# A bidirectional RWKV-7 scan on one Trainium2 core: the backward direction's token side moves to the other half of the partitions, and both directions alternate over four quadrants of TensorE

## The chip, the core and the metric

One core of a Trainium2 (trn2) chip runs the whole program. The metric is the time of one execution on the device in microseconds; the version with the lower median is the better one. All arithmetic is float32.

## What is computed

One layer of a diffusion backbone: adaLN-modulated RMSNorm, an input projection, grouped-query attention beside a bidirectional RWKV-7 time mixing, an output projection, and a mixture of experts. The change touches only the scan of the RWKV-7 part. Cut to it, the reference is:

```python
def rwkv7_scan(r, w, k, v, kk, b, s0, reverse):
    def step(S, inp):
        r_t, w_t, k_t, v_t, kk_t, b_t = inp
        sa = jnp.einsum('bhvk,bhk->bhv', S, kk_t)
        S = S * w_t[:, :, None, :] - sa[..., None] * b_t[:, :, None, :] + v_t[..., None] * k_t[:, :, None, :]
        return S, jnp.einsum('bhvk,bhk->bhv', S, r_t)
    ...
y_f, s_f = rwkv7_scan(..., s0[:, 0], False)      # forward
y_b, s_b = rwkv7_scan(..., s0[:, 1], True)       # backward
y = y_f + y_b
```

There are 8 heads of size 64, 128 context tokens and 512 latent tokens, and both directions run over both groups of tokens. The final states of the context tokens are an output.

## The kernel before

The program is a row of blocks that all engines enter together. In the trace the first block (projection) and the second (decays, attention) end at 427.6 us. The scan (lines 1145 to 1614) runs from there to 657.2 us; output projection, routing and experts follow.

**The chunked scan.** The 640 tokens are cut into 10 chunks of C = 64. Each of the ten steps (`STEPS`) treats one chunk of the forward direction (z = 0) and one of the backward direction (z = 1), for all 8 heads: head 2j + p lies in column group j (0 to 3) and partition half p (rows 64p to 64p + 63). Within a chunk the recurrence becomes products of 64 x 64 matrices and one triangular system:

- `gram` (L1290): products of B and of K with A and R, two per head, masked by DVE into `LR` (`lr_out`, L1550) and `MR` (`mr_out`, L1556)
- `turn_kb` (L1299): K and B transposed by a product with the identity, copied by ScalarE into `KB` (L1488)
- `right_sides` (L1340): A times the state plus MR times the values, copied by ScalarE into `RHc` (L1502)
- the triangular system, solved in two halves of 32 tokens: `by_inverse` (L1362), ScalarE's copy `U1` (L1505), `cross` (L1370), DVE's `RHd` (L1591), `by_inverse` again, ScalarE's copy `Uc` (L1513)
- `new_states` (L1381): KB times the values and times Uc; DVE adds the old state and multiplies by the decay (L1599, L1602)
- `outputs` (L1394): R times the state, MR times the values, LR times Uc; DVE adds them into `yacc` (L1609) or copies them (L1611)
- `inner` (L1310), DVE's `z_out` (L1562) and `inverse` (L1326): the inverse of the 32 x 32 triangular blocks of the next step, ScalarE's copy `XTf` (L1492). They need the inverses of the 16 x 16 diagonal blocks, which `diag_blocks` (L1277) gathers for two steps at a time and DVE solves row by row (`solve`, L1530, with `turn_diag` and `turn_back`, L1525 and L1543). Chunks are solved in groups of four, four and two: the first group before step 0, the others within steps 2 and 5.

**Where things lie.** A tile of TensorE is given by the rows that its operands occupy and the partitions that its result goes to. `half(z, p)` says in which half of the partitions the token side of head p lies. It returns p for both directions, so every product of 64 x 64 goes from rows 64p to partitions 64p: only the two quadrants on the diagonal of the array are used. PSUM has eight banks: BG1 = 0 and 1, BG2 = 2 and 3 (forward, backward), BLEV = 4, BDIAG = 5, BSER = 6 and 7.

**What sets the order.** There is no scheduler: each engine executes its list in the order in which it is written, and waits on semaphores. TensorE's list of a step (L1434 to L1473) is: right sides, Gram of B for the next step, first triangular product, Gram of K for the next step, cross, in steps 0, 1 and 4 the diagonal blocks of two more chunks, in step 2 the turned context states, inner for the next step, second triangular product, turned K and B for the next step, new states, outputs, inverse for the next step. Each of these loops treats the forward direction first and then the backward one. DVE's list of a step (L1577 to L1614) begins with `lr_out` of the next step and ends with the outputs; in steps 2 and 5 pieces of the solve stand between, the last piece and `turn_back` behind the outputs. SyncE loads what the next block needs when chunks are done: gates after step 1, half of the output weights after step 3, the bonus after step 4, the attention result after step 7. GpSimd only clears the zero state.

## Time and profile before

| what | value |
|---|---|
| median of 3 runs | 1206.3 us (1205.9 to 1213.83) |
| the profiled execution | 1203.15 us |
| its span, first to last instruction | 1201.3 us |
| mean granted TensorE clock | 0.923 of full speed |
| the scan with its preparation | 427.6 to 657.2 us |
| the ten steps | 458.3 to 657.2 us |

In the profile a matmul of float32 is two records (x2 of what the program issues), each with its weight load (PEld). The stretches below give for each engine the busy time and the number of records in that stretch: PE, PEld, DVE, ACT, POOL, then the granted clock of TensorE as a share of 2.4 GHz, the busy share of the DMA engines and their GB/s. A timeline merges instructions of one line that follow each other; its brackets say how long the engine was idle before and what ended that; "issue" is a wait for nothing that the profile shows.

### The profile page before, as it was taken

To read this page: it belongs to the slowest core of one execution; us is meant where nothing else is said; L and a number is where in the kernel's file an instruction comes from. 1 tells how busy PE (TensorE), PEld (TensorE's weight loads), DVE (VectorE), ACT (ScalarE), POOL (GpSimd) and SP (SyncE) were. 2 spreads that over 40 slices of the span, in tenths; PEclk is the share of its full clock that TensorE was granted. 3 is DMA by queue.
4 is the path that set the end of the run, shared out by engine and by line. 5 is a ranking of instruction groups with operands and counts; after the bars stand their busy time and mean duration, and the time that the engine had idled before them with its cause. 6 is when DMAs were issued, how large, how long until landed. Compare 5 with 4: busy or idle time off the path is not lost. (4 is left out here: it accounts for less than half of the span.)

```text
span 1201.3 us, 22681 instructions
## 1 busy us (share of the span) xinstructions
PE 1032.5 (86%) x9918; PEld 628.6 (52%) x9918; DVE 423.7 (35%) x887; ACT 268.0 (22%) x533; POOL 51.4 (4%) x73
## 2 busy tenths in 40 slices
PE   3699999979888747988899999299999999999960
PEld 0265555525666637887897555244444444444420
DVE  1402642231688653372833664500000010000007
ACT  2311222223676511221122212011111111111100
POOL 0330000010000000000000000300000000000003
PEclk9899999986899877988999999599999999999995
DMA  9713342549998010102101910696899898998816
GB/s 339 232 25 140 110 170 83 200 149 403 408 404 348 10 29 3 39 13 74 47 25 38 323 70 30 246 354 243 311 348 351 306 351 324 334 350 314 311 38 260
DMA packets 95926, 244.82 MB, mean 204 GB/s; under 512 B 6612, under 2 KB 11508, under 8 KB 95328
## 3 DMA queue, kind: packets, MB, share of 16 engines
q1 hardware_dynamic: 85664, 218.64, 50.0%
q0 software_dynamic: 4352, 11.34, 3.0%
q10 hardware_dynamic: 5824, 13.55, 2.9%
q8 instruction: 71, 1.16, 0.4%
q14 instruction: 15, 0.12, 0.0%
HBM read 176.51 MB, written 67.01 MB: 203 GB/s over the span
## 5 line engine op out<-in xcount | busy, mean ns | idle before, releaser
L2104 PE MATMUL ps<-arena 128*128 128x512 f32 x544 | 238.8, 596 | 1.7 <-ACT arena L2154 1.7
L2104 PEld LDWEIGHTS ps<-arena 128*128 128x128 f32 x544 | 102.3, 191 | 126.3 <-issue 125.6
L2118 PE MATMUL ps<-arena 128*128 128x512 f32 x272 | 121.1, 598 | 3.6 <-ACT arena L2158 3.6
L694 PE MATMUL ps<-arena 128*128 128x512 f32 (+3 forms) x448 | 123.6, 435 | 0.0
L694 PEld LDWEIGHTS ps<-arena 128*128 128x128 f32 (+1 forms) x448 | 67.7, 188 | 60.2 <-issue 59.3
L2118 PEld LDWEIGHTS ps<-arena 128*128 128x128 f32 x272 | 50.7, 191 | 61.9 <-issue 61.9
L1773 PE MATMUL ps<-arena 128*128 128x512 f32 x160 | 70.6, 593 | 0.9 <-PEq L1250 0.9
L561 DVE SCALAR_TENSOR_TENSOR arena<-arena 128x128 f32<-128x128 f32 (+3 forms) x56 | 30.9, 552 | 82.6 <-ACT arena L438 81.1
L2195 DVE TENSOR_TENSOR arena<-arena,ps 128x512 f32<-128x512 f32 x17 | 11.7, 689 | 135.5 <-ACT arena L2150 135.5
L2203 DVE COPY arena<-ps 128x512 f32<-128x512 f32 x17 | 11.8, 692 | 125.6 <-PE ps L2118 125.6
L628 PE MATMUL ps<-arena 128*128 128x512 f32 (+1 forms) x160 | 52.4, 485 | 0.0
L598 PE MATMUL ps<-arena 128*32 128x512 f32 x192 | 31.7, 705 | 23.9 <-DMA arena<-in_w_mod_dram 23.9
L2154 ACT ACTIVATE arena<-ps 128x1024 f32<-128x1024 f32 x18 | 18.4, 1024 | 139.9 <-PE ps L2096 139.9
L1773 PEld LDWEIGHTS ps<-arena 128*128 128x128 f32 x160 | 29.5, 189 | 34.8 <-issue 34.8
L2198 DVE TENSOR_TENSOR arena<-arena,ps 128x512 f32<-128x512 f32 x17 | 11.7, 689 | 94.6 <-PE ps L2104 94.6
L1295 PE MATMUL ps<-arena 64*64 64x128 f32 x640 | 40.4, 276 | 3.2 <-issue 3.2
L885 PE MATMUL ps<-arena 128*128 128x128 f32 x160 | 25.4, 291 | 20.1 <-DVE arena L1107 17.5
L628 PEld LDWEIGHTS ps<-arena 128*128 128x128 f32 x160 | 29.9, 189 | 21.5 <-issue 19.3
L1295 PEld LDWEIGHTS ps<-arena 64*64 64x64 f32 x640 | 35.9, 136 | 4.3 <-issue 3.4
L1321 PE MATMUL ps<-arena 32*32 32x32 f32 x640 | 11.6, 228 | 26.0 <-DVE arena L1548 16.1
L2163 ACT ACTIVATE arena<-ps 128x512 f32<-128x512 f32 x17 | 10.2, 597 | 103.0 <-PE ps L2118 103.0
L2096 PE MATMUL ps<-arena 128*128 128x128 f32 x144 | 19.6, 281 | 14.9 <-DMA arena<-gathered_tokens 14.9
(307 smaller groups left out, 1429.7 us busy)
## 6 DMA issues: line engine op xcount, KB each, us to landing
gathered_tokens<-arena SPq DMA_DIRECT2D x16, 2560.0 KB, 27.1
arena<-in_exp_up_dram SPq DMA_DIRECT2D x17, 2048.0 KB, 18.1
arena<-in_exp_gate_dram SPq DMA_DIRECT2D x17, 2048.0 KB, 13.1
arena<-in_exp_down_dram SPq DMA_DIRECT2D x17, 2048.0 KB, 9.8
arena<-in_w_mod_dram SPq DMA_DIRECT2D x12, 2048.0 KB, 13.8
arena<-gathered_tokens SPq DMA_DIRECT2D x18, 512.0 KB, 15.1
expert_outputs<-arena ACTq DMA_DIRECT2D x17, 512.0 KB, 8.1
arena<-in_w_in_dram SPq DMA_DIRECT2D x4, 2048.0 KB, 7.9
```

Source lines behind the costliest of these rows:

```text
L561: ins = dve.scalar_tensor_tensor(o[:, a:b], r_[:, base + off:base + off + b - a], mu[0:m, k, e:e + 1], o[:, a:b], ALU.mult, ALU.add)
L598: mm = pe.matmul(ps[32 * g:32 * g + 32, bank, :], cond32[:, k, :], ring[:, slot_of(what), k, :], start=(k < 4), stop=(k >= 4))
L628: mm = pe.matmul(ps[:, b + half, 0:w], hT[:, k, tt * P:(tt + 1) * P], ring[:, slot_of(("qkv", half)), k, 0:w], start=(k == 0), stop=(k == ...
L694: mm = pe.matmul(ps[0:m, b, 0:hi - lo], ring[:, slot_of(what), k, (e % 4) * P:(e % 4) * P + m], hT[:, k, lo:hi], start=(k == 0), stop=(k = ...
L885: mm = pe.transpose(ps[:, 4 + y // 4, (y % 4) * P:(y % 4 + 1) * P], prob[:, g, y * P:(y + 1) * P], ident)
L1295: mm = pe.matmul(ps[q:q + 64, bank + z, j * 2 * C:(j + 1) * 2 * C], kinds(k, z, s, j, p), kinds(A_, z, s, j, p, 2), start=True, stop=True)
L1773: mm = pe.matmul(ps[:, b, :], catT[k4][:, j, tt * P:(tt + 1) * P], wout[:, half, NC4 * k4 + j, :], start=(k4 == 0 and j == 0), stop=(k4 == ...
L2096: mm = pe.transpose(ps[:, XT0 + k // 4, (k % 4) * P:(k % 4 + 1) * P], xg[:, u, k * P:(k + 1) * P], ident)
L2104: mm = pe.matmul(ps[:, b, :], xgT[:, k, :], w[u][:, k, :], start=(k == 0), stop=(k == KT - 1))
L2118: mm = pe.matmul(ps[:, Y0 + half, :], hidT[:, k, :], wd[u][:, k, half * 512:(half + 1) * 512], start=(k == 0), stop=(k == 3))
L2154: act.activation(xgT, ps[:, XT0:XT0 + 2, :].rearrange("p b (k t) -> p (b k) t", t=P), ACT.Copy).then_inc(xgT_ok, 1)
L2203: dve.tensor_copy(yo[:, u, 512:], ps[:, Y0 + 1, :]).then_inc(yo_v, 1)
```

## The change

- `half(z, p)` becomes `p ^ z`: everything of the backward direction that has tokens on the partitions lies in the other half. Products from rows p to the token side, and from the token side to the state side, of the backward direction now use the two quadrants off the diagonal.
- `gram`, `turn_kb` and `new_states` run both directions in one loop over j, the two diagonal products first and then the two others.
- The right side of the backward direction is split: A times the state goes to BSER + 1; MR times the values is a piece of its own, `swapped_values`, written to BDIAG ahead of the inverse of the step before, copied by ScalarE to `MV1`, and added by DVE, as DVE's first instruction of a step.
- The outputs of the backward direction are split in the same way over two banks: DVE adds two pieces where it added one. Both directions' outputs alternate in one loop, and the backward ones are done two products before the forward ones.
- The values of the backward direction are copied to the other half by GpSimd's DMA queue, two DMAs a step into two buffers (`Vs`).
- Diagonal blocks write one bank for each direction, in steps 0, 1 and 4 the banks BG1 and BG1 + 1 in place of BDIAG, with waits for `lr_ok` before and `m_ok` behind.

```diff
         def half(z, p):
-            return p
+            return p ^ z
@@
         def values(z, s):
-            return vt[:, chunk_at(z, s)]
+            return Vs[s % 2] if z else vt[:, chunk_at(0, s)]
@@ gpsimd
                 pool.memset(states[0], 0.0).then_inc(zeroed, 1)
+                for s in range(STEPS):
+                    if s >= 2:
+                        pool.wait_ge(y_mm[1], s - 1)
+                    for p in range(2):
+                        pool.dma_start(rows(Vs[s % 2], half(1, p)), rows(vt, p)[:, chunk_at(1, s)]).then_inc(ld_vs[s % 2], 16)
@@ tensor: gram (turn_kb and new_states alike)
-                    for z in range(2):
-                        for j in range(NC4):
+                    for j in range(NC4):
+                        for z in range(2):
                             for p in range(2):
@@ tensor: right_sides
-                        V = values(z, s)
-                        for j in range(NC4):
...
-                        mm.then_inc(rhs_mm[z], 1)
+                    V0 = values(0, s)
+                    for j in range(NC4):
+                        cols = slice(j * C, (j + 1) * C)
+                        for p in range(2):
+                            pe.matmul(ps[64 * p:64 * p + 64, BSER, cols], kinds(A_, 0, s, j, p), rows(S, p)[:, 0, j], start=True, stop=False)
+                        for p in range(2):
+                            q = half(1, p)
+                            mm = pe.matmul(ps[64 * q:64 * q + 64, BSER + 1, cols], kinds(A_, 1, s, j, p), rows(S, p)[:, 1, j],
+                                           start=True, stop=True)
+                        if j == NC4 - 1:
+                            mm.then_inc(rhs_mm[1], 1)
+                        for p in range(2):
+                            mm = pe.matmul(ps[64 * p:64 * p + 64, BSER, cols], rows(MR[s % 2], p)[:, 0, j, 0], rows(V0, p)[:, j],
+                                           start=False, stop=True)
+                    mm.then_inc(rhs_mm[0], 1)
+
+                def swapped_values(s):
+                    pe.wait_ge(mr_ok[1], s + 1)
+                    pe.wait_ge(ld_vs[s % 2], 32 * (s // 2) + 32)
+                    if s:
+                        pe.wait_ge(rh_ok[1], s)
+                    V1 = values(1, s)
+                    for j in range(NC4):
+                        for q in range(2):
+                            mm = pe.matmul(ps[64 * q:64 * q + 64, BDIAG, j * C:(j + 1) * C], rows(MR[s % 2], q)[:, 1, j, 0], rows(V1, q)[:, j],
+                                           start=True, stop=True)
+                    mm.then_inc(mv_mm, 1)
@@ tensor: a step
                     outputs(s)
                     if more:
+                        if s == 2:
+                            pe.wait_ge(so_ok, 1)
+                        swapped_values(s + 1)
                         inverse(s + 1)
@@ scalar: a step
-                    for z in range(2):
-                        act.wait_ge(rhs_mm[z], s + 1)
-                        act.activation(RHc[:, z], quarter(BSER + z), ACT.Copy).then_inc(rh_ok[z], 1)
+                    act.wait_ge(rhs_mm[0], s + 1)
+                    act.activation(RHc[:, 0], quarter(BSER), ACT.Copy).then_inc(rh_ok[0], 1)
@@ vector: a step
+                    dve.wait_ge(rhs_mm[1], s + 1)
+                    dve.wait_ge(mv_ok, s + 1)
+                    dve.tensor_tensor(RHc[:, 1], MV1, quarter(BSER + 1), ALU.add).then_inc(rh_ok[1], 1)
                     if s == 2:
                         turn_diag(1)
```

**TensorE, the head of step 0 and of its right sides.** In the kernel before, the inverse (L1335) is followed by right sides, whose state part is L1354 and whose value part L1358, a pair for each direction and column group:

```order
L1321 MATMUL ps<-arena 32x32 x32
L1335 MATMUL ps<-arena 32x32 x32
L1354 MATMUL ps<-arena 64x64 x2
L1358 MATMUL ps<-arena 64x64 x2
L1354 MATMUL ps<-arena 64x64 x2
```

In the changed kernel inner is L1336, the inverse L1350, the value part of the backward direction L1389, and in right sides L1369 is the forward state part, L1372 the backward one, L1377 the forward value part:

```order
L1336 MATMUL ps<-arena 32x32 x32
L1350 MATMUL ps<-arena 32x32 x32
L1389 MATMUL ps<-arena 64x64 x8
L1369 MATMUL ps<-arena 64x64 x2
L1372 MATMUL ps<-arena 64x64 x2
L1377 MATMUL ps<-arena 64x64 x2
```

The eight backward value products left the loop and stand in front of it; the four groups of three that remain hold 24 products where eight pairs of two held 32.

**DVE, one step.** Before, a step begins with the masks (L1553, L1559) behind the `z_out` (L1564) of the preparation and ends with two outputs (L1611):

```order
L1564 TENSOR_TENSOR arena<-ps,arena 128x256
L1553 TENSOR_TENSOR arena<-ps,arena 128x512 x2
L1559 TENSOR_TENSOR arena<-ps,arena 128x512 x2
L1591 TENSOR_TENSOR arena<-arena,ps 128x256 x2
```

Now the same masks (L1614, L1620) stand behind the sum that makes the backward right side (L1643):

```order
L1625 TENSOR_TENSOR arena<-ps,arena 128x256
L1643 TENSOR_TENSOR arena<-arena,ps 128x256
L1614 TENSOR_TENSOR arena<-ps,arena 128x512 x2
L1620 TENSOR_TENSOR arena<-ps,arena 128x512 x2
L1655 TENSOR_TENSOR arena<-arena,ps 128x256 x2
```

The right side of the backward direction is now behind whatever DVE still has of the step before, and ahead of the masks.

## Rows read from the trace of the kernel before

**Rows 1.** Busy time by stretch, one row for each step of the scan (0 to 9).
```profile
458.30:481.65 23.35, 21.86 (x712) 20.86 (x704) 6.40 (x13) 4.70 (x10) 0.00 (x0) 0.84 0.01 4
481.65:502.95 21.30, 19.84 (x710) 18.75 (x704) 6.88 (x14) 4.81 (x10) 0.00 (x0) 0.92 0.02 5
502.95:521.20 18.25, 18.21 (x614) 17.25 (x608) 13.15 (x46) 4.36 (x10) 0.00 (x0) 1.00 0.25 75
521.20:543.85 22.65, 18.76 (x584) 17.71 (x576) 15.20 (x29) 3.78 (x9) 0.00 (x0) 0.85 0.03 8
543.85:570.60 26.75, 22.29 (x711) 20.85 (x704) 7.04 (x14) 4.74 (x10) 0.00 (x0) 0.81 0.30 79
570.60:587.95 17.35, 16.80 (x584) 15.94 (x576) 13.08 (x46) 3.72 (x9) 0.00 (x0) 1.00 0.22 79
587.95:611.30 23.35, 19.66 (x583) 18.51 (x576) 15.23 (x29) 3.78 (x9) 0.00 (x0) 0.85 0.01 4
611.30:629.30 18.00, 17.16 (x584) 16.16 (x576) 6.39 (x13) 3.67 (x9) 0.00 (x0) 1.00 0.06 11
629.30:647.50 18.20, 16.90 (x584) 16.04 (x576) 6.39 (x13) 3.77 (x9) 0.00 (x0) 1.00 0.17 70
647.50:657.20 9.70, 8.81 (x264) 7.88 (x256) 1.48 (x4) 2.69 (x7) 0.00 (x0) 1.00 0.01 3
```

**Rows 2.** Timeline of TensorE (PEld: weight loads): start us, us, engine, line, idle before.
```profile
629.32 0.19 PEld L1354 LDWEIGHTS ps<-arena 64*64 64x64 f32 x4
629.43 0.20 PEld L1358 LDWEIGHTS ps<-arena 64*64 64x64 f32 x4
...
631.18 1.73 PEld L1295 LDWEIGHTS ps<-arena 64*64 64x64 f32 x32
...
622.73 2.08 PE L1390 MATMUL ps<-arena 64*64 64x64 f32 x64
```

**Rows 3.** The same view at three gaps of the weight loads.
```profile
470.47 0.92 PEld L1321 LDWEIGHTS ps<-arena 32*32 32x32 f32 x62 [1.58 <-issue]
...
629.09 0.15 PEld L1335 LDWEIGHTS ps<-arena 32*32 32x32 f32 x7 [0.70 <-issue]
...
633.08 0.51 PEld L1366 LDWEIGHTS ps<-arena 32*32 32x32 f32 x23 [0.17 <-issue]
635.05 0.33 PEld L1366 LDWEIGHTS ps<-arena 32*32 32x32 f32 x9 [1.46 <-issue]
```

**Rows 4.** DMA: GB/s in 40 slices of 466-476, 630-648; queue q8; the attention load.
```profile
GB/s 0 0 0 0 0 0 0 66 0 0 0 0 0 0 0 0 0 0 0 0 0 0 66 0 0 0 0 0 0 0 0 0 0 0 0 0 0 0 66 0
...
q8 instruction: 46, 0.75, 1.5%
...
GB/s 432 410 364 432 410 114 36 0 0 0 0 0 0 36 0 0 0 0 0 0 0 36 0 0 0 0 0 0 0 36 0 0 0 0 0 0 0 18 36 0
...
arena<-attn_scratch SPq DMA_DIRECT2D x1, 1280.0 KB, 5.6
```

**Rows 5.** Costliest groups of the page, and the loads of diagonal blocks in step 0.
```profile
L2104 PE MATMUL ps<-arena 128*128 128x512 f32 x544 | 238.8, 596 | 1.7 <-ACT arena L2154 1.7
...
L598 PE MATMUL ps<-arena 128*32 128x512 f32 x192 | 31.7, 705 | 23.9 <-DMA arena<-in_w_mod_dram 23.9
...
467.50 1.21 PEld L1285 LDWEIGHTS ps<-arena 64*32 64x32 f32 x128
```

**Rows 6.** Timeline of DVE and TensorE in step 3, around the end of the solve.
```profile
529.62 1.25 DVE L1548 STREAM_TRANSPOSE arena<-arena 128x1024 f32<-128x1024 f32 x1
...
542.95 0.42 DVE L1611 COPY arena<-ps 128x256 f32<-128x256 f32 x1 [0.98 <-PE ps L1408]
...
532.30 1.11 PE L1321 MATMUL ps<-arena 32*32 32x32 f32 x64 [3.68 <-DVE arena L1553]
...
535.05 3.18 PE L1306 MATMUL ps<-arena 64*64 64x64 f32 x64
```

More of the change, by code:

```diff
@@ L1177, in build @@
         Zc = place_tile(2, NC4, 32)
+        Vs = [place_tile(NC4, C) for _ in range(2)]
+        MV1 = place_tile(NC4, C)
+        mv_mm, mv_ok = sem("mv_mm"), sem("mv_ok")
+        ld_vs, y_part = [sem("ld_swapped_0"), sem("ld_swapped_1")], sem("y_part")
         def diagonal(v):
@@ L1399, in outputs @@
                             pe.wait_ge(mr_ok[z], s + 2)
-                        V = values(z, s)
-                        for j in range(NC4):
-                            for p in range(2):
-                                pe.matmul(ps[64 * p:64 * p + 64, BG2 + z, j * C:(j + 1) * C], kinds(R_, z, s, j, p), rows(S, p)[:, z, j],
-                                          start=True, stop=False)
-                            for k, src in ((MR, V), (LR, Uc[:, z])):
-                                for p in range(2):
-                                    q = half(z, p)
-                                    mm = pe.matmul(ps[64 * p:64 * p + 64, BG2 + z, j * C:(j + 1) * C], rows(k[s % 2], q)[:, z, j, 1],
-                                                   rows(src, q)[:, j], start=False, stop=(k is LR))
@@ L1453, in _ @@
                         first = s + 4 + (s % 4)
-                        pe.wait_ge(m_ok, 2 if s == 0 else 3 if s == 1 else 4)
+                        for z in range(2):
+                            pe.wait_ge(lr_ok[z], s + 2)
                         for e in range(2):
-                            diag_blocks(first + e, BDIAG, e)
+                            diag_blocks(first + e, (BG1, BG1 + 1), e)
                     if s == 2:
```

108 lines of the change are left out of this document (75 added, 33 removed).

## The prediction

> **What bounds the kernel now.** I read three views, in this order. First the table of busy time by stretch, cut at the starts of the scan's steps [rows 1]: the ten steps run from 458.3 to 657.2 us, and in the plain steps (2, 5, 7, 8) TensorE's matmul records cover 93 to 100% of 17.4 to 18.3 us. Steps 0, 1 and 4 also make diagonal blocks (704 weight loads where a plain step has 576), and in steps 3 and 6 TensorE idles although nothing was added. Then the timeline inside the steps, for what a matmul costs [rows 2] and where it stops [rows 3], and last the DMA view of the same stretches, because a few of TensorE's gaps have no engine as releaser.
>
> That last view shows a limit that the busy share hides. A step issues 576 weight loads and 576 matmuls [rows 1]. Between the two unexplained gaps at 629.1 and 635.1 us stand 7 + 64 + 32 + 23 = 126 weight loads (the 64 are sixteen rows of right sides like the two shown), with their matmuls about 252 instructions [rows 2, 3]: one 16 KB packet of queue q8, of which the scan fetches 46 [rows 4] for about 11,900 instructions (46 x 256 = 11,800). The first bandwidth row of [rows 4] has forty slices of 0.25 us; a packet stands in the eighth, from 467.75 us. The loads that stop soon after 468.7 [rows 5] go on at 470.47 [rows 3], 2.5 to 2.7 us after it began, and the next packet stands at 471.5, 1.0 to 1.3 us after that. The gap that ends at 635.05 gives 1.9 to 2.4 and 0.8 to 1.3 with the second bandwidth row (slices of 0.45 us from 630). So once TensorE is at the end of what it holds, 256 instructions cost about 1.1 + 2.45 = 3.55 us, whatever they are. I call that a page; a plain step has 1,163 / 256 = 4.54 of them (1,152 and eleven waits). At 18.0 us a step takes 3.96 us a page, only 0.4 above this floor. No two packets of these rows stand closer than seven or eight slices of 0.45 us in the second, 3.2 to 3.6 us.
>
> **The change part by part.** Quadrants. Now two quadrants work at a time: four records of right sides (two matmuls, each in two passes) take 0.11 to 0.12 us [rows 2], 29 ns a pass of 64 columns, and 32 passes of 128 columns take 1.73 us, 55 ns each. The change gives the backward direction the other two quadrants and alternates. Do quadrants that share input rows overlap? Two rows say yes. Four column strips fed by the same 128 rows make 192 passes of 512 columns in 31.7 us, 165 ns each, where a full-width pass of 512 takes 238.8 / 544 = 439 [rows 5]. The diagonal blocks, four tiles in two row groups, load 128 times in 1.21 us, 9.5 ns a pass of 32 columns [rows 5]; at two tiles a time the rate of 128 columns would make that 14. So I halve the pure array time where both directions take part:
> - two Gram products, 1.76 each, to 0.88: 1.76 saved
> - turned K and B, 1.87 to 0.94: 0.93
> - new states, 1.87 to 0.94: 0.93
> - outputs: 96 passes of 29 ns, 2.80; of six pairs for both directions, four stay in the old quadrants, 1.87: 0.93
> - right sides, 1.87: two of four pairs stay in the old quadrants, one goes beside them, one moves to the new piece before the inverse, 0.94 + 0.47: 0.46
>
> That is 5.0 us of TensorE time a step. Inner, inverse, cross and the triangular products stay on the block diagonal and gain nothing.
>
> The Trainium skill, "TensorE: Matmul & The Clock Gate", section on packing small matmuls, says that a weight load overlaps running matmuls only when its row group differs. The new neighbours share their row group, so by that sentence most of the 5.0 us would stay. The two rows just given speak against it, and the measurement decides; the case is kept as a rival.
>
> The floor. The number of instructions is unchanged: every matmul that leaves one loop stands in another. So a plain step cannot fall to 13.0 us; it falls to 4.54 x 3.55 = 16.1. Here the Trainium skill, "Runtime: NRT & Kernel Launch", section on instruction fetch, says that crossing a 16 KB boundary is mostly hidden. By the rows it is hidden only while 256 instructions take longer than 3.55 us, which this change ends. Its sentence would give the second case below.
>
> Steps, gains in us against [rows 1]:
> - 0 and 1: 1,163 + 256 = 1,419 instructions, 5.54 pages, 19.7 each; step 0 begins at half clock, so I take 20.0: 3.3 and 1.6
> - 4: it took 26.75 where 5.54 pages at 3.96 are 21.9; the 4.8 above that falls beside the load of the output weights, which I take to hold a packet up, and carry over: 24.5, so 2.2
> - 2 (with the turned states, 64 more): 4.8 pages, 17.0: 1.2. 5: 16.1: 1.2
> - 7: 16.1: 1.9
> - 8: TensorE enters a page at 629.09, but the next packet comes in the seventh slice of the second row of [rows 4], at 632.7 instead of 630.2, behind the attention load of 1.25 MB: 16.1 plus 2.6 is 18.7, a loss of 0.5
> - 3 and 6: DVE is still solving when the step begins; its last transpose ends at 530.87 and TensorE resumes at 532.30 [rows 6], 11.5 us before the step's end. In the new order the first DVE instruction of a step is the sum that makes the backward right side, so TensorE stands one stage earlier, before the backward triangular product, with that, a Gram product, cross, inner and all the rest (about 930 instructions, 3.6 pages, two of them already held) behind it. Counted from DVE's release the old order needs 13.0 us (two of them because the turned K and B ran at half clock, 3.18 for 64 passes where new states take 2.08 at full [rows 2, 6]); the new one I put at 11 to 12.5: 1.0 each, with -1.5 and +3 as ends
> - 9: right sides and outputs -1.9, one more addition by DVE after them (0.42 [rows 6]): 1.3
> - ahead of step 0: the value part of the first backward right side stands between inverse and right sides: -0.5
>
> Waits that the change adds. The backward right side is DVE's instead of ScalarE's, 0.42 by the nearest row, an addition of the same size [rows 6]: nothing in a plain step, DVE is busy 6.4 of 18 us [rows 1]. Outputs of the backward direction need a second addition, 0.42, behind outputs that end together; what is queued behind them is the right sides of the next step. Three additions and their hand-overs take about 1.4 us from the last output, and TensorE has 0.47 (value part) + 1.0 (inverse) to do meanwhile: covered to within 0.1, and inside a page's 3.55. The GpSimd queue now copies the backward values across the halves, two 64 KB DMAs a step, due two steps later: hidden for their users; but they share the DMA engines with the code packets. No row shows that price. Below: nothing; above: the 1.25 MB load delays a packet by 2.6 us, a twentieth of the bytes in each of ten steps by perhaps 0.3. I take 1.5 in all.
>
> Sum: 3.3 + 1.6 + 1.2 + 1.0 + 2.2 + 1.2 + 1.0 + 1.9 - 0.5 + 1.3 - 0.5 = 13.7, less 1.5 = 12.2. The profiled execution took 1203.15 us (span 1201.3), so 1190.9 for one like it; the median shown is 3.15 above it, 1206.3, and the forecast for a median is 1206.3 - 12.2 = 1194.
>
> **Rivals.**
> 1. No floor. If the code queue can run ahead once TensorE asks faster, the array time decides: 5.0 in each of steps 0, 1, 4, 7, 8, but only about 2.3 in steps 2 and 5, where DVE's own 13 us [rows 1] with its waits fill 15 to 16, then 2 each in 3 and 6 and 0.8 for the ends: 34, time 1172. For it: most page crossings show no gap. Against it: both gaps read above end about 2.5 us after a packet starts, and no two packets in [rows 4] stand closer than 3.2.
> 2. Slower: quadrants with the same input rows do not overlap. Array time stays, and the joint loops now finish both directions at the end, so every hand-over is later: the wait before the second triangular product (0.3) and small ones, 0.5 a step; in steps 3 and 6 a Gram product of 1.76 and the products before it move behind DVE's solve, 2 each; 5 + 4 = 9, time 1215. It decides once the two new quadrants add more than two thirds of their old time. Against it: the strips and the diagonal blocks of [rows 5].
> 3. The clock. TensorE at 1.2 GHz is not rare here: the granted clock is 0.81 to 0.85 in steps 0, 3, 4 and 6, after each of the long gaps, and 1.00 in steps 7 and 8 [rows 1]. A TensorE that waits for code idles about a quarter of the time, so it may fall more often. Its joint products (0.94 + 1.76 + 0.94 + 0.94 + 1.87 + 0.47) then cost 6.9 us more a step, 13.0 + 6.9 = 19.9 against a floor of 16.1. Over the scan, whose steps 0, 3, 4 and 6 already hold such stretches, that is some 30 if all of it is at half clock, 1224, and 15 for half of it, 1209. From about two fifths on it undoes the gain.
> 4. The change does not do what it says, because the order in the queue puts two products for the same quadrants behind each other (outputs end with two such pairs, and the next column begins with one). That is in the sum: four pairs of six.
>
> **How the numbers follow.** The forecast's case has 0.62, from 1185 (a page of 3.3 us: 46 x 0.25 = 11 more, less what is bound otherwise) to 1204 (steps 3 and 6 at their bad ends, 2 us more from late packets). No floor 0.12, no overlap 0.08, clock at half for half or more of the scan 0.12, other new waits 0.06. A measurement of this kernel tells about 1%, 12 us, from no change. Faster by over 1% is the lower half of the forecast's case and all of the first rival, together 0.48; slower by over 1%, above 1218, takes the worst of the clock and part of the second rival, 0.08; the rest, 0.44, is within 1%. The range 1176 to 1212 leaves out most of the first rival and half of the second and third.
>
> **What would show it.** In the changed kernel's profile: 46 or 47 code packets in the scan again, 3.4 to 3.7 us apart almost without exception, and gaps of 0.5 to 1.5 us without a releaser at most of them; plain steps of 16 to 16.5 us; turned K and B and new states in about 1.0 us instead of 2.08; step 3 with DVE released before the backward triangular product; the busy share of TensorE in steps 7 and 8 down to about three quarters. Plain steps of 13 to 14 us would refute the floor, 64 passes in 2 us the overlap, a granted clock near 0.75 in steps 7 and 8 the assumption on the clock, and steps 3 and 6 longer than 24 us my reading of the moved sum.

## The result and the profile after

The changed kernel takes 1210.4 us (median of 20 runs, 1204.9 to 1217.6) where the kernel before takes 1206.3 (20 runs, 1200.8 to 1213.9): ratio 1.0043, 95% interval 1.0026 to 1.0059. The forecast was 1194. The change costs 4 us; it does not gain 12.

The ten steps of the scan in the changed kernel, the table of [rows 1]: stretch, its length, then busy time (and instructions) of TensorE's matmuls, its weight loads, DVE, ACT and GpSimd, the granted clock, DMA share and GB/s.

```profile
458.30:479.25 20.95, 17.48 (x708) 16.06 (x704) 6.97 (x15) 4.97 (x11) 1.03 (x2) 0.77 0.04 10
479.25:499.20 19.95, 15.71 (x707) 14.05 (x704) 6.96 (x15) 4.72 (x11) 1.03 (x2) 0.91 0.04 14
499.20:517.75 18.55, 14.21 (x608) 12.69 (x609) 15.20 (x51) 4.21 (x10) 1.03 (x2) 1.00 0.27 80
517.75:541.00 23.25, 16.48 (x580) 14.90 (x576) 15.00 (x28) 3.79 (x9) 1.03 (x2) 0.71 0.05 12
541.00:567.60 26.60, 15.95 (x706) 14.21 (x705) 7.09 (x15) 4.59 (x10) 1.03 (x2) 0.86 0.42 114
567.60:588.10 20.50, 15.63 (x576) 13.95 (x576) 14.52 (x49) 3.73 (x9) 1.03 (x2) 0.77 0.11 35
588.10:611.90 23.80, 16.36 (x582) 14.96 (x577) 15.79 (x30) 3.79 (x10) 1.03 (x2) 0.71 0.03 6
611.90:629.50 17.60, 14.31 (x576) 13.03 (x576) 6.96 (x15) 3.56 (x9) 1.03 (x2) 0.90 0.12 29
629.50:649.05 19.55, 16.13 (x582) 14.88 (x577) 6.96 (x15) 3.79 (x10) 0.00 (x0) 0.74 0.16 59
649.05:660.60 11.55, 9.28 (x240) 8.16 (x240) 1.30 (x4) 2.30 (x6) 0.00 (x0) 0.64 0.01 3
```

Two things show at once. TensorE's busy time fell in each of steps 0 to 8 (step 7: 17.16 to 14.31; only step 9 rose, 8.81 to 9.28), yet steps 7 and 8 take 17.6 and 19.55 us, against 18.0 and 18.2. Over the whole scan, busy time and code packets of the two kernels (first the kernel before, then the changed one, which also has the row of queue q8 for the same stretch):

```profile
458.30:657.00 198.70, 180.29 (x5864) 169.95 (x5856) 91.05 (x217) 40.02 (x92) 0.00 (x0) 0.91 0.11 34
```
```profile
458.30:660.50 202.20, 151.51 (x5844) 136.90 (x5840) 96.73 (x234) 39.45 (x92) 8.22 (x16) 0.80 0.13 39
...
q8 instruction: 46, 0.75, 1.5%
```

28.8 us of TensorE's busy time are gone, the instructions (but for 20 of 5,864 matmul records) and the 46 packets are the same, and the scan is not shorter. Where did 28.8 us go? For the most part into gaps without a releaser. Step 7's weight loads show the pattern of [rows 3] (start, duration, idle time before):

```profile
612.39 0.19 PEld L1369 LDWEIGHTS ps<-arena 64*64 64x64 f32 x3
613.60 0.13 PEld L1372 LDWEIGHTS ps<-arena 64*64 64x64 f32 x1 [1.01 <-issue]
...
619.75 0.31 PEld L1320 LDWEIGHTS ps<-arena 64*64 64x64 f32 x12
621.55 1.46 PEld L1320 LDWEIGHTS ps<-arena 64*64 64x64 f32 x50 [1.48 <-issue]
...
627.56 0.46 PEld L1350 LDWEIGHTS ps<-arena 32*32 32x32 f32 x26
628.83 0.58 PEld L1350 LDWEIGHTS ps<-arena 32*32 32x32 f32 x38 [0.81 <-issue]
```

I counted them in the whole scan: a gap of over 0.25 us in TensorE's starts that ends 1.5 to 3.4 us after a packet of q8 begins. The kernel before has 12 such gaps at its 46 packets, 13.2 us in all from start to start; the changed one has 32, 43.7 us in all. 30.5 us more of gaps stand against 28.8 us less work. They do not stand there by chance: of the 48 gaps of over 0.25 us in the changed kernel's scan, 31 end between 2.0 and 3.0 us after a packet begins. Packets begin 3.85 us apart in the median before and 3.94 after.

Outside the scan there are two further losses. Ahead of step 0 (rows of the kernel before, then of the changed one; inverse, then what follows):

```profile
457.27 1.11 PE L1335 MATMUL ps<-arena 32*32 32x32 f32 x64 [0.55 <-DVE arena L1564]
458.31 0.48 PE L1354 MATMUL ps<-arena 64*64 64x64 f32 x4
```
```profile
456.35 1.11 PE L1350 MATMUL ps<-arena 32*32 32x32 f32 x64 [0.54 <-DVE arena L1625]
457.39 1.01 PE L1389 MATMUL ps<-arena 64*64 64x64 f32 x14
458.10 0.37 PE L1372 MATMUL ps<-arena 64*64 64x64 f32 x2
...
458.30 0.42 PE L1369 MATMUL ps<-arena 64*64 64x64 f32 x4
```

The value part (L1389) stands between inverse and right sides, whose forward part starts 1.95 us after the inverse instead of 1.04. And behind the last outputs (TensorE and DVE of the kernel before, then of the changed one):

```profile
656.54 0.40 PE L1408 MATMUL ps<-arena 64*64 64x64 f32 x8
657.89 1.96 PE L1773 MATMUL ps<-arena 128*128 128x512 f32 x4 [0.94 <-PEq L1250]
...
656.99 0.42 DVE L1609 TENSOR_TENSOR arena<-arena,ps 128x256 f32<-128x256 f32 x1 [0.98 <-PE ps L1408]
```
```profile
660.09 0.42 PE L1453 MATMUL ps<-arena 64*64 64x64 f32 x4
662.45 2.90 PE L1846 MATMUL ps<-arena 128*128 128x512 f32 x3 [1.93 <-PEq L1257]
...
660.57 0.42 DVE L1674 TENSOR_TENSOR arena<-arena,ps 128x256 f32<-128x256 f32 x1 [5.74 <-PE ps L1453]
661.09 0.42 DVE L1680 TENSOR_TENSOR arena<-arena,ps 128x256 f32<-128x256 f32 x1
661.55 0.42 DVE L1684 TENSOR_TENSOR arena<-arena,ps 128x256 f32<-128x256 f32 x1
```

Three additions instead of one now stand between the last outputs and the next stage: TensorE idles 1.93 us instead of 0.94. The stage then begins with three matmul records in 2.90 us where four took 1.96: the granted clock is 0.50 there.

### The profile page after: what moved, and what is told of

It is laid out like the page before. It is cut to its first block and busy times, and to the rows that moved or that the text cites. A ratio compares the mean times of both kernels' runs of the same rounds, so it can differ in the third digit from the quotient of the medians.

```text
span 1208.7 us, 22775 instructions
## 1 busy us (share of the span) xinstructions
PE 1007.8 (83%) x9918; PEld 598.5 (50%) x9918; DVE 430.6 (36%) x907; ACT 267.6 (22%) x533; POOL 61.7 (5%) x93
## 5 line engine op out<-in xcount | busy, mean ns | idle before, releaser
L2268 DVE TENSOR_TENSOR arena<-arena,ps 128x512 f32<-128x512 f32 x17 | 11.7, 689 | 135.5 <-ACT arena L2223 135.5
L2276 DVE COPY arena<-ps 128x512 f32<-128x512 f32 x17 | 11.8, 692 | 127.2 <-PE ps L2191 127.2
L2271 DVE TENSOR_TENSOR arena<-arena,ps 128x512 f32<-128x512 f32 x17 | 11.7, 689 | 94.6 <-PE ps L2177 94.6
L1397 PE MATMUL ps<-arena 32*32 32x64 f32 x640 | 24.9, 253 | 20.3 <-DVE arena L1643 12.1
L628 PEld LDWEIGHTS ps<-arena 128*128 128x128 f32 x160 | 30.1, 190 | 21.2 <-issue 19.3
L1307 PE MATMUL ps<-arena 64*64 64x128 f32 x640 | 30.7, 337 | 6.5 <-issue 6.5
L1397 PEld LDWEIGHTS ps<-arena 32*32 32x32 f32 x640 | 20.5, 127 | 23.5 <-DVE arena L1643 12.5
## 6 DMA issues: line engine op xcount, KB each, us to landing
arena<-in_exp_up_dram SPq DMA_DIRECT2D x17, 2048.0 KB, 18.2
```

What stands on the lines that cost most here:

```text
L628: mm = pe.matmul(ps[:, b + half, 0:w], hT[:, k, tt * P:(tt + 1) * P], ring[:, slot_of(("qkv", half)), k, 0:w], start=(k == 0), stop=(k == ...
L1307: mm = pe.matmul(ps[q:q + 64, bank + z, j * 2 * C:(j + 1) * 2 * C], kinds(k, z, s, j, p), kinds(A_, z, s, j, p, 2), start=True, stop=True)
L1397: mm = pe.matmul(ps[q:q + 32, BSER + z, j * C:(j + 1) * C], block32(XTf[s % 2], p, b)[:, z, j], block32(src, p, b)[:, z, j], start=True, s ...
```

## The experiments

All scans below run from the first right side of step 0 to the last outputs, in one trace per kernel. Where part of the computation is left out, the expectation says which.

**The same two kernels again.** They tell how far a single trace can be trusted, so they stand first, though they ran last.

> The changed kernel once more, for a second trace. Theory: scan 202.2 again within 2 us, its step 5 between 20 and 21, its 46 packets 3.9 apart in the median, about 32 of them with a gap; the stage from 305 to 420 us may take 7 us longer, since that has two courses. If the scan differs by more than 3 us, comparisons by single traces do not carry the 3.5 us between the kernels.

> The kernel before once more, for a second trace. Theory: scan 198.7 within 2 us, plain steps 17.4 to 18.3, its 46 packets 3.85 apart in the median, about 12 with a gap.

> The changed kernel a third time. Two traces and its close variants have the scan at 200 to 204. Theory, no gain in the scan and 3.4 us outside it: scan 200 to 203; from the first matmul behind the attention blocks to the first right side 38.2 us (36.9 in the kernel before), and from the last outputs to the first matmul of the next stage 1.9 us (0.9 before). Rival, the scan itself is the loss: it stands 3 us or more above the kernel before in this pair too.

> The kernel before a third time; its scan was 198.7 and 203.2. Theory: between these, that is within 3 us of the changed kernel's, and 36.9 and 0.9 us for the two stretches outside. Rival: 199 or below again, so that 203.2 was the exception.

The scan rows of the kernel before (second, third trace), then of the changed one:

```profile
458.50:661.70 203.20, 180.37 (x5861) 169.02 (x5856) 91.25 (x217) 40.09 (x92) 0.00 (x0) 0.93 0.11 33
```
```profile
459.60:660.20 200.60, 181.40 (x5864) 170.09 (x5856) 91.17 (x217) 40.09 (x92) 0.00 (x0) 0.92 0.12 34
```
```profile
460.10:660.70 200.60, 146.39 (x5844) 131.77 (x5838) 96.69 (x235) 39.36 (x92) 8.23 (x16) 0.84 0.14 39
```
```profile
464.00:666.00 202.00, 152.18 (x5844) 137.29 (x5838) 96.77 (x234) 39.61 (x92) 8.23 (x16) 0.80 0.14 39
```

| stretch, us | before (3 traces) | changed (3 traces) | difference of means |
|---|---|---|---|
| first matmul of L938 (the last of the attention block) to first right side | 36.9, 37.2, 37.9 | 38.2, 38.3, 38.4 | +1.0 |
| scan | 198.7, 203.2, 200.6 | 202.2, 200.6, 202.0 | +0.8 |
| last outputs to next matmul | 0.9, 0.9, 0.9 | 1.9, 1.9, 1.9 | +1.0 |
| from there to the 64x64 products | 7.1, 7.1, 7.1 | 8.7, 7.1, 8.8 | +1.1 |

The sum is 3.9 us, and the medians differ by 4.1. The scans are not ordered: the trace shown before the prediction was the shortest of three, and the second, 203.2 us, lies 2.5 us outside what was expected of it. The stretches behind the scan repeat to 0.1 us in the kernel before; the one ahead spreads over 1.0. Mean lengths of the steps 0 to 9: before 23.0, 22.0, 18.8, 23.0, 25.8, 19.3, 23.2, 17.8, 18.9, 9.1; changed 20.6, 20.3, 19.1, 23.6, 25.9, 20.7, 23.7, 17.4, 19.5, 10.7. Step 9 is worth a look, since its 1.6 us are more than the scan's whole difference. Its three lengths in the changed kernel are 11.4, 8.9 and 11.7 us. The first is the last row of the table at the top, at a granted clock of 0.64; the other two:

```profile
651.70:660.70 9.00, 6.25 (x240) 5.41 (x240) 1.24 (x4) 2.15 (x6) 0.00 (x0) 1.00 0.02 4
```
```profile
654.30:666.00 11.70, 9.23 (x240) 8.07 (x240) 1.27 (x3) 2.27 (x6) 0.00 (x0) 0.65 0.01 3
```

At full clock the step takes what it takes in the kernel before (8.8 to 9.5 us in its three traces, to the last outputs); at a granted 0.64 and 0.65 it takes 2.4 and 2.7 us more than at 1.00. All eleven traces of the changed kernel and of its variants with as many instructions say the same: 8.4 to 8.9 us in the three with 0.98 to 1.00 in this step, 11.0 to 11.8 in the eight with 0.50 to 0.75, none between. The two traces with the long step 9 have the slow start of the next stage too (8.7 and 8.8 us for 7.1).

Packets stand 3.85, 4.00 and 3.93 us apart in the medians before, 3.94, 3.85 and 3.80 after; gaps at them are 12, 16, 15 against 32, 36, 33. Two packets that both have a gap stand 3.86, 3.85 and 3.80 us apart in the changed kernel, and two that both have none 3.85, 4.03 and 3.97 in the kernel before. So in the kernel before TensorE's own work sets most distances, in the changed one the packets do, and 256 instructions come out at nearly the same time.

Not all of the idle time is the packets'. In the means of three traces, TensorE's idle time that ends 1.5 to 3.4 us after a packet begins rose from 12.8 to 37.0 us, and the rest of it from 7.3 to 14.5. Six of those 7 us are in steps 3 and 6: TensorE waits 5.0 to 5.8 and 7.0 to 7.1 us there for the moved sum (L1643), where it waited 2.9 to 3.7 and 3.0 to 3.3 us for the masks. Step 3 of the changed kernel, TensorE and then DVE:

```profile
526.66 1.06 PE L1397 MATMUL ps<-arena 32*32 32x64 f32 x16 [5.02 <-DVE arena L1643]
...
525.05 1.25 DVE L1609 STREAM_TRANSPOSE arena<-arena 128x1024 f32<-128x1024 f32 x1
526.22 0.38 DVE L1643 TENSOR_TENSOR arena<-arena,ps 128x256 f32<-128x256 f32 x1
```

**Fewer instructions** (floor or array time?), in both kernels; the first line below is in both edits, the second is the changed kernel's, and the product of K with the values in new states goes too:

```diff
-                        for i, k in enumerate((K_, B_)):
+                        for i, k in ((1, B_),):
...
-                            pe.matmul(ps[64 * p:64 * p + 64, BG2, cols], rows(MR[s % 2], p)[:, 0, j, 1], rows(V0, p)[:, j], start=False, stop=False)
```

> The changed kernel without the turned K, its product with the values in new states, and the products of MR with the values in the outputs (left out of the computation): 192 instructions a step fewer, 0.75 of a page, and about 1.9 us less array time. Theory, floor: a plain step falls by 0.75 x 3.75 = 2.8 us, to 14.8, and the whole by 20 to 28 us (1183 to 1190). Rival, array time decides: at most 1.9 a step, and since the array is already idle between, 8 to 14 us (1197 to 1203).

> The kernel before with the same products left out: 192 instructions fewer, 3.7 us less array time a step. Theory, floor: a plain step of 18.0 falls to 3.8 pages x 3.75 = 14.3, as in the changed kernel's twin, so that the two differ by less than 4 us; the whole some 22 to 30 us less (1177 to 1185). Rival, array time decides in the kernel before and something else in the changed one: this one falls by 3.7 a step, over 30 us, and stands well below the changed kernel's twin.

First the changed kernel's twin, then that of the kernel before:

```profile
466.70:642.50 175.80, 132.97 (x4948) 119.69 (x4944) 96.56 (x234) 39.16 (x92) 8.23 (x16) 0.80 0.15 44
```
```profile
456.00:630.80 174.80, 154.02 (x4964) 143.83 (x4960) 90.20 (x217) 39.50 (x92) 0.00 (x0) 0.90 0.13 38
```

The scans fall by 25.8 and 26.0 us against the means of three, to within 1.0 us of each other, although TensorE is busy 21 us less in the first. Both lost some 1,790 instructions (of both columns), 7.0 pages, 3.7 us a page. In the changed kernel the busy time fell by 17 us and the scan by 26, so there the instructions decide and not the array. In the kernel before the busy time fell by 26.7 us, as much as the scan, so its run cannot tell the two apart. The totals, 1230.4 and 1221.5 where 1183 to 1190 and 1177 to 1185 were expected, say nothing of the scan: with other outputs TensorE has 1,638 instead of 1,516 matmul records behind it, and that part takes some 44 us more in both.

**Narrower products**, meant to take array time away at the same count:

```diff
-                                                    rows(src, q)[:, j], start=(i == 0), stop=(i == 1))
+                                                    rows(src, q)[:, j, 0:16], start=(i == 0), stop=(i == 1))
```

> The changed kernel with new states and outputs 16 instead of 64 columns wide (steps s >= 0, both directions); the other columns of the outputs and states are not computed. Same number of instructions. It takes about 0.9 us (new states) and some 1.4 us (outputs) of array time out of each step. Theory, a floor of about 3.75 us for each 256 instructions: the plain steps stay within 0.3 us of 17.6 and 19.6, the whole within 3 us of the changed kernel (1207 to 1213). Rival, array time and hand-overs decide: about 1.5 to 2.3 us less in each of seven steps, 1195 to 1200.

> The kernel before with the same two products 16 columns wide. Array time falls by about 1.4 (new states) and 2.1 us (outputs) a step, 3.5 in all. Theory, floor: a plain step of 18.0 falls only to its pages, 17.3 to 17.6, and with shorter steps 3 and 6 the whole gains 3 to 8 us (1198 to 1203). Rival, array time decides in the kernel before: 3 us in each of seven steps, about 1185.

It did not take any away: at full clock the 64 passes of new states start within 1.79 us in the kernel before's twin at 16 columns, 1.81 at 64. What changed is the clock: 0.70 over the changed kernel's scan (0.80 to 0.84 before), with 164.8 us busy, and 0.82 in the other (0.91 to 0.93), with 196.3. The first scan stays at 203.3; the second grows to 210.3. The totals are 1216.1 and 1225.9, both above what was expected (1207 to 1213, 1198 to 1203). An unplanned reading, of one trace each: where packets pace TensorE a slower clock disappears in their gaps (15 us more busy, 2 more time), and where TensorE fills them most of it is paid (16 more busy, 9.5 more time). Neither was what the experiment was for.

**Direction after direction**, the alternation undone:

```diff
-                    for j in range(NC4):
-                        for z in range(2):
+                    for z in range(2):
+                        for j in range(NC4):
```

> The changed kernel with Gram products, turned K and B and new states made direction after direction again (the backward direction still in its own quadrants), so that only two quadrants work at a time there: 2.7 us more array time a step, and nothing left out. Theory, floor: plain steps within 0.5 us of 17.6 to 18.5, the scan within 3 us of 202.2, perhaps shorter, since hand-overs come earlier and TensorE's clock stays up. Rival, the alternation is worth its array time: 1.5 to 2.7 us longer in each of seven steps, the scan at 213 to 220.

The scan takes 203.5 us with TensorE busy 162.2 instead of 151.5: the alternation saves 11 us of array time and 1 to 3 us of the scan, within the spread of single traces. The total is 1215.3 (ratio to the kernel before 1.0086, 1.0050 to 1.0121); how much of the 5 us above the changed kernel is the alternation's is open: in its profiled run the stretch described in the last section took its long course. That quadrants overlap is not in doubt: turned K and B, 64 passes at full clock, start within 0.94 us (step 5 of the changed kernel) and within 1.69 here.

**The value part behind the inverse:**

```diff
+                        inverse(s + 1)
                         swapped_values(s + 1)
-                        inverse(s + 1)
```

> The changed kernel with the value part of the backward right side behind the inverse instead of in front of it (and ScalarE's two copies in the same order); nothing is left out. Theory, floor: the place of eight products changes nothing in a plain step, which enters its pages at the same rate; DVE's sum is ready 0.5 to 1 us later, which a page gap covers: scan 201 to 205. Rival, the early part saves a hand-over: 1 us a step, 10 us in all, scan at 212.

ScalarE's two copies change places in the same way. Scan 200.1, total 1210.7 (ratio 1.0036, 1.0010 to 1.0062), where the changed kernel has 200.6 to 202.2 and 1210.4. The early place is worth nothing either.

**The GpSimd copies:**

> The changed kernel with the copies of the backward values across the halves only for steps 0 and 1 (the later steps reuse these; their true values are left out), so 16 of the 20 copies of 64 KB are gone. Theory, the copies cost little: the scan within 2 us of 202.2. Rival, they delay the instruction packets in each step: 8 steps x 0.5 to 1 us, the scan at 194 to 198. What lies after the scan may do other work, since the values differ, so the scan is to be compared and not the total.

Scan 199.5: 1 to 3 us less, where I had put 1.5 in the sum. With a spread of that size the run bounds their price and does not measure it. The total, 1210.7, did not move.

**The loads of the scan:**

```diff
-                sp.wait_ge(y_mm[0], steps_until(0, 0, 4))
+                sp.wait_ge(y_mm[0], STEPS)
+                sp.wait_ge(y_mm[1], STEPS)
...
                 load_wout(sp, 0)
-                sp.wait_ge(y_mm[1], steps_until(1, 7, NCH))
```

> The changed kernel with all loads that the scan issues for later use (gate, output weights, bonus, attention) issued after its last outputs instead. Theory, late instruction packets behind these loads cost about 5.6 us in step 4, 2.5 to 3 in step 5, 2 in step 8: the scan falls from 202.2 to 191 to 194 us, of which the part after it gives back what the loads no longer hide (the whole may come out slower). Rival, the clock or hand-overs make these steps long: steps 4, 5 and 8 keep their lengths within 1 us.

> The kernel before with the same loads issued after the scan. Theory, there a late packet was felt only in step 4 (4 to 5 us); steps 5, 7 and 8 keep 17.3, 18.0 and 18.2 within 0.4 us, and the scan falls from 198.9 to about 194, so that before and changed kernel stand level without the loads. Rival: no change in step 4.

Steps 4, 5 and 8 of the changed kernel without loads:

```profile
544.10:565.40 21.30, 18.09 (x709) 16.66 (x709) 6.96 (x15) 4.70 (x10) 1.03 (x2) 0.76 0.05 11
565.40:583.40 18.00, 14.40 (x577) 12.92 (x577) 15.04 (x50) 3.62 (x9) 1.03 (x2) 0.91 0.05 11
...
623.20:639.90 16.70, 12.63 (x586) 11.33 (x581) 6.96 (x15) 3.62 (x10) 0.00 (x0) 1.00 0.02 5
```

They fall by 4.6, 2.7 and 2.8 us against the means; the scans by 10.0 (to 191.6) and 7.1 (to 193.7). In the kernel before step 4 falls by 4.2, and step 8, which was expected to keep its 18.2 us, takes 17.0. With the loads, step 5 of the changed kernel has a gap of 2.47 us where 0.8 to 1.5 are usual; the second fence shows the DMA rate there, forty slices of 0.375 us from 565:

```profile
571.73 0.29 PEld L1377 LDWEIGHTS ps<-arena 64*64 64x64 f32 x3 [2.47 <-issue]
```
```profile
GB/s 137 82 300 382 382 410 437 410 382 306 284 22 0 0 0 0 0 0 0 0 0 0 0 44 0 0 0 0 0 0 0 0 0 0 0 44 0 0 0 0
```

The bonus load ends at about 569.3. In the trace the packet that follows it begins at 569.04, 5.7 us after the one before (563.31), and TensorE goes on 2.7 us after its begin. In step 8 it is the same: the attention load moves from 627.94 to 632.68, and packets begin at 626.34 and 632.87. In the kernel before this is a matter of luck: step 5 took 17.3, 20.8 and 19.8 us in three traces, in the changed one 20.5, 20.4 and 21.3. Issued late the loads are given back: 563 to 564 us behind the scan instead of 544 to 548, totals 1218.7 and 1218.2.

**The loads cut into parts** of 128 to 160 KB, one outstanding at a time:

```diff
-                sp.dma_start(attnX.rearrange("p a t -> p (a t)"), attn_d).then_inc(ld_at, 16)
+                for n in range(8):
+                    if n:
+                        sp.wait_ge(ld_at, 16 * n)
+                    sp.dma_start(attnX.rearrange("p a t -> p (a t)")[:, 320 * n:320 * n + 320], attn_d[:, 320 * n:320 * n + 320]).then_inc(ld_at, 16)
```

> The changed kernel with the loads of the output weights (2 MB), bonus and attention (1.25 MB each) cut into 16, 8 and 8 parts, each issued by SyncE when the one before has landed, from the same points of the scan on. Nothing else is changed and nothing is left out. Theory, an instruction packet waits behind what of a load stands before it in the DMA engines: with one part of 128 KB outstanding it waits under 1 us instead of 2 to 6, so step 4 falls from 26.6 to about 21.5, step 5 from 20.5 to 18, step 8 from 19.6 to 17 to 18; the scan from 202.2 to 192 to 195, and since the loads still land within the scan nothing is given back: 1200 to 1203. Rival, packets are delayed by the loads' share of the engines however it is cut: the scan stays within 3 us of 202.

> The kernel before with the same loads cut in the same way. Theory: only step 4 (26.8) falls, to about 21.6 as it did without the loads, the scan from 198.9 to about 194, the total by 5 to 1201. So the two kernels come out level within 3 us, and what the change lost is the packets that its shorter steps no longer cover. Rival: step 4 unchanged, total 1206.

Scans 195.0 and 193.0, totals 1205.4 and 1201.4: 5 us less for each kernel, nothing given back behind the scan. With 12 runs each, the kernel before so cut is 0.36% faster than uncut (0.9964, 0.9929 to 0.9999), and the changed one level with before (0.9993). Steps 4 are 22.2 and 23.0; step 8 of the changed kernel stayed at 19.9, and its packets, beside the parts of the load, stand 3.7 to 5.2 us apart: not every packet is freed.

**DVE's block solve.** First only its last piece moved behind the next step's sum, the term "sum in front of the masks":

```diff
+                    last = todo.get(s - 1, [])
+                    if last:
+                        solve(*last[2])
+                        turn_back(last[2][0])
...
-                    if pieces:
-                        solve(*pieces[2])
-                        turn_back(pieces[2][0])
```

> The changed kernel with the last piece of DVE's block solve and its turn back moved behind the next step's sum that makes the backward right side. Theory, the moved sum keeps TensorE waiting 5.2 us in step 3 and 7.3 us in step 6: both waits go, the time comes back partly as a later wait for the turned blocks, and steps 3 and 6 fall by 2 to 4 us each (to 20 to 21.5), the whole by 4 to 8 us (1203 to 1206). Rival, those steps are bound by instruction pages or by the solve's own chain anyway: under 1 us each, the whole unchanged at 1210.

A miss: total 1214.0 where 1203 to 1206 was expected, steps 3 and 6 at 24.9 and 23.5. The triangular product starts at once, but the masks and the turned blocks are still behind the solve, and TensorE then waits for those. First TensorE, then DVE in step 3:

```profile
523.88 0.91 PE L1407 MATMUL ps<-arena 32*32 32x64 f32 x32
531.54 0.69 PE L1336 MATMUL ps<-arena 32*32 32x32 f32 x25 [6.75 <-DVE arena L1614]
...
528.86 1.25 DVE L1609 STREAM_TRANSPOSE arena<-arena 128x1024 f32<-128x1024 f32 x1
530.03 1.25 DVE L1614 TENSOR_TENSOR arena<-ps,arena 128x512 f32<-128x512 f32 x2
```

The last transpose of the solve (L1609) ends at 530.1, and the masks (L1614) come only then. Moving a wait is not removing it. Then the solve spread over three steps, from step 1 and 4 on, together with the cut loads:

```diff
+                    todo[s0, 1], todo[s0, 2] = [(0, 0), (1, 2)], [(2, 6)]
+                    todo[s0 + 1, 0], todo[s0 + 1, 1], todo[s0 + 1, 2] = [(6, 8)], [(8, 12)], [(12, 15)]
+                    todo[s0 + 2, 0], todo[s0 + 2, 1] = [(15, 16)], [(16, 17)]
```

(The numbers are rows of the solve; 0 stands for the first transpose, 16 for the turn back.)

> The changed kernel with the cut loads, and with DVE's block solve (15 rows and the turn back) spread over three steps in place of one: it starts in step 1 and 4, where DVE idles, and its turn back comes before the products that need it in steps 3 and 6. Theory: beyond the gain of the cut loads, steps 3 and 6 fall from 23.3 and 23.8 to 18 to 20, since TensorE no longer waits behind a solve: another 6 to 10 us, total 1192 to 1197. Rival, the pages or another wait take over in steps 3 and 6 as they did when only the last piece was moved: under 3 us beyond the cut loads.

> The kernel before with the cut loads and with DVE's block solve spread over three steps. Theory: TensorE's waits behind the solve in steps 3 and 6 go here too, so the scan falls from 193.0 with the cut loads alone to 184 to 187, and the total by 6 to 9 to 1193 to 1196. That is no longer than the changed kernel with the same two edits (scan 188.3, total 1199.9): with stalls and late packets gone both stand on the instruction pages. Rival, the four quadrants pay once the other waits are gone: this kernel 4 us or more above 1200.

Steps 3 and 6 of the changed kernel, now with 11.5 us of DVE in them instead of 15:

```profile
523.40:544.90 21.50, 14.53 (x576) 13.28 (x577) 11.58 (x20) 3.29 (x8) 1.03 (x2) 0.84 0.05 16
586.90:605.10 18.20, 14.04 (x580) 12.75 (x581) 11.54 (x20) 3.36 (x9) 1.03 (x2) 0.92 0.26 73
```

Totals 1199.9 (0.9944, 0.9918 to 0.9969) and 1200.3 (0.9947, 0.9924 to 0.9970), both faster than the kernel before by about 7 us and level with each other. The scans are 188.3 and 192.4; whether those 4 us are the quadrants' or the trace's is open. Step 6 fell in both kernels, to 18.2 and 18.0. Step 3 did not in the kernel before (23.1), and in the changed one TensorE still waits 5.31 us for DVE in it. For the kernel before the solve added 1 us to the cut loads, not the 6 to 9 I expected: its steps 0 and 1 took 24.4 and 23.1 in this trace.

## Why the prediction was wrong

Point by point, in its own order.

- *Quadrants that share input rows overlap*: right. 1.86 to 0.94 us for the 64 passes of turned K and B at full clock. The Trainium skill, "TensorE: Matmul & The Clock Gate", section on packing small matmuls, would have a weight load overlap only with another row group; the rows here disagree with it.
- *The number of instructions is unchanged, 46 packets, gaps at most of them*: right, 46 and 32 to 36. But packets were to stand 3.4 to 3.7 us apart and plain steps to take 16 to 16.5: neither came, which is the next point.
- *"256 instructions cost about 1.1 + 2.45 = 3.55 us"*: **this is the step that failed.** The 2.45 is right (packet to resumption, medians of 2.3 to 2.7 in the twenty traces). The 1.1 was the short end: at the gaps of the changed kernel's three traces, from resumption to the next packet took 1.25 to 1.39 us in the medians. Packets that both have a gap stand 3.80 to 3.86 apart, all of them 3.80 to 3.94. The prediction read the 3.96 us a page of a plain step as 0.4 above the floor; the room was 0.1 to 0.2. The kernel before was mostly bound by its array (busy 17.16 of 18.0 us in step 7), but the packets stood just below, and the array time taken away laid them bare. At 4.54 pages a plain step costs 17.3 to 17.9 us by the medians, not 16.1, and that is what step 7 takes (17.4 in the mean of three, 17.8 before). 46 pages by 0.3 are 14 us, more than the whole forecast gain. I read the price from two gaps where 46 packet distances were there to be taken: a median over the scan would have given 3.85.
- *Steps 0 and 1*: 2.4 and 1.6 gained of 3.3 and 1.6, nearly right. They had 4.15 and 3.97 us a page before, so something was left to gain. These are the only steps that gained over 1 us.
- *Steps 2, 5 and 7, 1.2, 1.2 and 1.9*: -0.3, -1.4 and +0.3. Step 5's packet is late behind the bonus load, and surely so now; I had seen this only for steps 4 and 8.
- *Step 4, 2.2*: nothing. I carried the 4.8 us beside the load over unchanged and took the gain from the rest. Without loads the step takes 21.3 and 21.6 us in the two kernels, 5.54 pages by 3.85: the rest was at the floor, and the load costs 4 to 5 us in either.
- *Step 8, -0.5*: -0.6, right, also in its cause (the late packet at 632.87; 16.7 us without the loads).
- *Steps 3 and 6, 1.0 each*: -0.6 and -0.5, inside the ends given there (-1.5 and +3). The mechanism came as described: DVE's sum releases TensorE before the backward triangular product. Its size was wrong. From the end of DVE's last transpose to the end of the step the new order was to need 11 to 12.5 us; it needs 14.2 to 15.3, the old one 13.0 to 14.2. Of the old order's 13.0 the text laid two to the half clock of the turned K and B, where its rows show 3.18 against 2.08, which is 1.1.
- *Step 9, 1.3*: -1.6 in the mean, the clock's work: level with the kernel before at full clock, 2.5 us longer at 0.64. The step holds two packets and otherwise a chain of products and hand-overs, so nothing covers slow products.
- *Ahead of step 0, -0.5*: -1.0. Of this 0.9 is the value part in front; the rest is within the spread. *Behind the scan*: not in the sum, -2.1, half of it the three additions in a row that the text had named as covered, which they are only while a next step follows.
- *Copies, 1.5 in all*: 1 to 3, consistent, no more. The two copies of a step are 128 KB, a tenth of the 1.25 MB load and not the twentieth that the text has; by its own rule they would be 2.6 in all. The row that it calls an addition of 0.42 is a copy (L1611); the additions take 0.42 as well.
- *Rivals*: no floor is refuted by the gaps; no overlap is refuted by 0.94; rival 3's clock came (0.80 to 0.84 over the scan, 0.91 to 0.93 before). Its price in the paced steps is small (2 us in the scan with narrower products), but where no packet paces it is paid: 1.6 us in step 9 and 1.1 behind the scan, in the mean. Why the clock falls more is shown only so far: TensorE idles more.

So the gain of 12 became a scan level within its spread, and the 3.9 us of the table are 2.0 of added work at the two ends (value part, additions), 2.7 of clock in step 9 and behind it, and 0.8 gained in the other nine steps together. These are means of three traces whose scans differ by 4.5 us, so the split is shown in its signs better than in its tenths. That 1210.4 lies in the range 1176 to 1212 is luck: the case that the sum describes ends at 1204, and what filled the distance was in part not in it. Faster by over 1% had 0.48, within 1% had 0.44.

## What to carry to other kernels

When TensorE runs hundreds of small products without a loop, count instructions before array time: here 256 of them cost 3.8 to 3.9 us, and 29 us less array time at the same number moved nothing, while 1,790 fewer saved 26 us. Take such a price as a median over all packets of the stretch, not from the two gaps that show it best, and let a plain step's own time per page stand as the floor unless gaps prove room below it. What saves array time there leaves TensorE idle more, and its clock may be at half just where the chain is bare again. Loads that are issued within such a stretch are worth cutting, with one part outstanding: that gave 5 us in either kernel. And look at what a moved instruction waits behind: DVE's sum, moved to the front of a step, kept TensorE idle for 5 and 7 us, where it had been 3, in the two steps in which DVE was late.

## What I had not expected of the hardware

The stretch between 305 and 428 us, ahead of the scan and the same code in all kernels, has two courses. From the first matmul of L850 to the first diagonal block it takes 122.1 us in thirteen of the 20 traces and 125.5 to 127.9 in seven. Ten microseconds of it in the changed kernel with cut loads, then in that with cut loads and spread solve:

```profile
304.80:314.80 10.00, 7.51 (x45) 5.77 (x46) 5.27 (x11) 6.70 (x14) 0.00 (x0) 0.83 1.03 409
```
```profile
306.60:316.60 10.00, 7.52 (x34) 6.66 (x35) 3.73 (x9) 5.76 (x13) 0.00 (x0) 0.50 1.02 404
```

The granted clock is 0.83 in one and 0.50 in the other, with 45 and 34 matmuls done. The seven long ones are of variants of both kernels, one of the changed kernel itself, and all have a granted clock of 0.50 or 0.51 in those first 10 us, the others 0.83 or 0.84. It can explain a part of why single runs spread over 13 us, and a difference of 4 needed 20 runs of each. The clock also fell (0.80 to 0.70 and 0.92 to 0.82) when products had 16 columns instead of 64, although TensorE had the same instructions and its records were busy for longer.
